# One last column unit by output halves with its column sums inside, tables, parameters and first weight unit ahead, two remainders in quarters

## The reference

```
for l in range(DEPTH):                               # DEPTH = 2
    mod = c_act @ ada_w[l] + ada_b[l]
    sh1, sc1, g1, sh2, sc2, g2 = split(mod, 6)
    h = rms_norm(x, norm1_g[l]) * (1.0 + sc1) + sh1                    # norm 1
    x = x + g1 * token_mixer(h, ..., w_in[l], ..., w_out[l])
    h = rms_norm(x, norm2_g[l]) * (1.0 + sc2) + sh2                    # norm 2
    x = x + g2 * conv_ffn(h, ffn_up[l], ..., ffn_down[l])
return rms_norm(x, final_g)
```

## Time and profile before

| what | value |
|---|---|
| median of 3 runs | 1697.12 us (1693.07 to 1697.74) |
| span of the profiled execution | 1696.2 us |
| PE busy | 1544.1 us (91%) |
| DVE busy | 718.4 us (42%) |
| ACT busy | 533.5 us (31%) |
| POOL busy | 641.6 us (38%) |
| mean granted TensorE clock | 0.946 |

### The profile page before, as it was taken

The page is one execution under the profiler, slowest core; times in us unless marked ns, Lnnn a source line. Parts: engine busy times, 40 slices in busy tenths (PEclk is TensorE's granted clock), DMA queues, the critical chain, the costliest instruction groups (busy, mean ns, idle before and its releaser), DMA issues.

```text
span 1696.2 us, 20273 instructions
## 1 busy us (share of the span) xinstructions
PE 1544.1 (91%) x7414; PEld 1222.0 (72%) x7414; DVE 718.4 (42%) x1051; ACT 533.5 (31%) x665; POOL 641.6 (38%) x283
## 2 busy tenths in 40 slices
PE   5698897899989999999968889789997999999998
PEld 5576785556868888888856778655576888888886
DVE  4879635534341122332158872654354212224211
ACT  2221332344333433321122123334442443333112
POOL 3323222211435555545513322231115455555451
PEclk7799998999979999999979989989998999999998
DMA  8575111000123333464248431100002333345431
GB/s 315 185 234 185 58 50 51 1 1 1 50 69 91 92 96 99 124 212 139 71 150 294 134 122 50 50 26 0 1 26 75 89 90 94 99 124 168 164 115 50
DMA packets 188828, 171.60 MB, mean 101 GB/s; under 512 B 15717, under 2 KB 151365, under 8 KB 188741
## 3 DMA queue, kind: packets, MB, share of 16 engines
q1 hardware_dynamic: 187572, 170.22, 31.9%
q10 hardware_dynamic: 1169, 0.25, 0.1%
HBM read 168.35 MB, written 2.10 MB: 100 GB/s over the span
## 4 chain that ended last, share of the span: by engine, by line
issue 34%; PE 25%; POOL 17%; DVE 17%; POOLq 3%; DVEq 1%; DMA 1%; ACT 1%; ACTq 0%; SPq 0%
POOL w_lo L517 13%; DVE asum L958 10%; PE psum L1361 7%; PE psum L1363 7%; PE psum L1362 7%; POOL hid_lo L584 3%; PE psum L1482 1%; PE psum L1504 1%; POOLq L569 1%; POOLq L538 1%; POOLq L570 1%; PE psum L1339 1%; POOL qm L556 1%; POOLq L533 1%; DVE asum L956 1%
## 5 line engine op out<-in xcount | busy, mean ns | idle before, releaser
L517 POOL TENSOR_TENSOR w_lo<-w_raw,w_hi 128x2048 fp32r<-128x2048 f32 x76 | 354.3, 4662 | 530.4 <-ACT w_hi L648 528.9
L648 ACT ACTIVATE w_hi<-w_raw 128x2048 fp32r<-128x2048 f32 (+2 forms) x104 | 192.9, 1855 | 652.2 <-PE psum L1363 555.9
L1361 PE MATMUL psum<-h_hi,w_hi 128*128 128x512 f32 x960 | 380.9, 397 | 5.7 <-DVE h_lo L932 4.8
L1362 PE MATMUL psum<-h_lo,w_hi 128*128 128x512 f32 x960 | 376.3, 392 | 0.0
L1363 PE MATMUL psum<-h_hi,w_lo 128*128 128x512 f32 x960 | 376.2, 392 | 0.0
L1361 PEld LDWEIGHTS psum<-h_hi,w_hi 128*128 128x128 f32 x960 | 182.1, 190 | 48.1 <-DVE h_lo L932 7.9
L1363 PEld LDWEIGHTS psum<-h_hi,w_lo 128*128 128x128 f32 x960 | 181.8, 189 | 38.8
L1362 PEld LDWEIGHTS psum<-h_lo,w_hi 128*128 128x128 f32 x960 | 182.0, 190 | 36.5
L522 POOL TENSOR_TENSOR w_lo<-w_raw,w_hi 128x1792 fp32r<-128x1792 f32 (+2 forms) x28 | 114.3, 4081 | 165.2 <-ACT w_hi L648 165.2
L1285 DVE SCALAR_TENSOR_TENSOR fy<-psum,par,fy 128x511 f32<-128x511 f32 x44 | 33.0, 750 | 325.5 <-ACT fy L840 325.5
L1363 PE MATMUL psum<-hid_hi,w_lo 128*128 128x512 f32 x352 | 140.4, 399 | 0.0
(11 more groups left out here) (234 smaller groups left out, 2139.6 us busy)
## 6 DMA issues: line engine op xcount, KB each, us to landing
w_raw<-in_ffn_up SPq DMA_DIRECT2D x88, 512.0 KB, 5.0
a_raw<-in_ada_w SPq DMA_DIRECT2D x34, 1024.0 KB, 6.6
w_raw<-in_w_in SPq DMA_DIRECT2D x48, 512.0 KB, 4.6
a_mix<-in_ada_w SPq DMA_DIRECT2D x18, 1024.0 KB, 5.3
w_raw<-in_ffn_down SPq DMA_DIRECT2D x32, 512.0 KB, 4.4
w_raw<-in_w_out SPq DMA_DIRECT2D x16, 512.0 KB, 3.9
w_raw<-in_ffn_down SPq DMA_DIRECT2D x16, 384.0 KB, 3.1
w_raw<-in_w_in SPq DMA_DIRECT2D x4, 560.0 KB, 5.2
```

The costliest lines, as they stand in the source:

```text
L517: g.tensor_tensor(w_lo[:, slot_of(u), :], w_raw[:, slot_of(u), :], w_hi[:, u % HI, :].bitcast(F32), ALU.subtract).then_inc(s_lo, 1)
L648: s.activation(w_hi[:, u % HI, 0:n], w_raw[:, r, 0:n], ACT.Copy).then_inc(s_hi, 1)
L1361: m(ps, l_hi, r_hi, start=first, stop=False)
L1362: m(ps, l_hi, r_lo, start=False, stop=False)
```

## The change

- The last unit of w_out and of ffn_down (`last_unit`) makes output half 0 for all k, signals `s_half`, and then half 1. Inside half 1 stand the column sums of the squares of chunks 0 to 5 (ahead of its last three k) and of chunk 6 (ahead of its last k). `x_update` takes chunk 6 on `s_half`.
- `sqrt_table` stands ahead of `last_squares`, no longer behind it. Unit 0 of the next layer is rounded (`high(l + 1, 0)`) and its remainder made (`low(l + 1, 0)`) ahead of the last squares.
- Units 1 and 19 are rounded inside `norm_high`, ahead of the fourth chunk (19 stood between the squares and the root, 1 behind the norm). Their remainders are made in four pieces of 512 columns with a drain between (`low_by_quarters`).
- The next layer's `parameters` are set ahead of the last update.
- In the units that follow a norm, TensorE makes the two products with `h_hi` as soon as that is there, and the third one when `h_lo` is.
- The loop over layers is written out on all engines; the inner loops stay.

```diff
+            def low_by_quarters(l, u):
+                pool.wait_ge(s_hi, l * UNITS + u + 1)
+                for i in range(4):
+                    at = slice(i * T, (i + 1) * T)
+                    last = g.tensor_tensor(w_lo[:, slot_of(u), at], w_raw[:, slot_of(u), at],
+                                           w_hi[:, u % HI, at].bitcast(F32), ALU.subtract)
+                    if i < 3:
+                        pool.drain()
+                last.then_inc(s_lo, 1)
...
-            with pool.Fori(0, L) as l:
-                low(l, 0)
+            low(0, 0)
+            for l in range(L):
                 pool.wait_ge(s_ss, 2 * l + 1)
-                low(l, 1)
+                low_by_quarters(l, 1)
...
-                low(l, 19)
+                low_by_quarters(l, 19)
...
+                if l + 1 < L:
+                    low(l + 1, 0)
...
-            def norm_high(chunks, shift):
+            def norm_high(chunks, shift, l, u):
                 for c8 in range(KD):
+                    if c8 == 3:
+                        high(l, u)
                     act.wait_ge(s_hm, chunks + c8 + 1)
...
+                sqrt_table()
                 last_squares(KD + 2 * KD * l, 2 * l + 1)
-                high(l, 19)
                 norm_root(2 * l + 1)
-                norm_high(2 * KD * l + KD, 24)
+                norm_high(2 * KD * l + KD, 24, l, 19)
...
+                if l + 1 < L:
+                    high(l + 1, 0)
+                sqrt_table()
                 last_squares(2 * KD + 2 * KD * l, 2 * l + 2, l * (AUNITS // 2) + (AUNITS + EARLY) // 2)
...
-            def x_update(l, gate, ada=None):
+            def x_update(l, gate, ada=None, ahead=None):
                 for q in range(4):
+                    if q == 3 and ahead is not None:
+                        ahead()
...
-                    unit_used(dve, l, U_OUT + q if gate == 16 else U_DOWN + 3 * q + 2)
+                    if q == 3:
+                        dve.wait_ge(s_half, 2 * l + (1 if gate == 16 else 2))
+                    else:
+                        unit_used(dve, l, U_OUT + q if gate == 16 else U_DOWN + 3 * q + 2)
                     for e in range(2):
                         c8 = 2 * q + e
+                        if c8 == KD - 1:
+                            unit_used(dve, l, U_OUT + 3 if gate == 16 else UNITS - 1)
...
-                x_update(l, 40, ada)
+                x_update(l, 40, ada, (lambda: parameters(l + 1)) if l + 1 < L else None)
...
+            def last_unit(u, banks, nk, rhs, first, n):
+                for e in range(2):
+                    for kk in range(nk):
+                        if e == 1 and kk == nk - 3:
+                            sum_squares(n, (0,))
+                        if e == 1 and kk == nk - 1:
+                            sum_squares(n, (1,))
+                        at = kk * 256 + e * P
+                        hi, lo = rhs(kk)
+                        ins = three(banks[e], w_hi[:, u % HI, at:at + P], w_lo[:, slot_of(u), at:at + P], hi, lo,
+                                    first and kk == 0, kk == nk - 1)
+                    ins.then_inc(s_used if e else s_half, 1)
+                sum_squares(n, (2,))
...
                         if f == 0:
+                            pe.wait_ge(s_hhi, l * 2 * KD + KD + kk + 1)
+                            for e in range(2):
+                                at = kk * 256 + e * P
+                                ps = pair(f % 3)[e]
+                                m(ps, w_hi[:, f % HI, at:at + P], h_hi[:, kk, :], start=kk == 0, stop=False)
+                                m(ps, w_lo[:, f % RAW, at:at + P], h_hi[:, kk, :], start=False, stop=False)
                             pe.wait_ge(s_hlo, l * 2 * KD + KD + kk + 1)
```

More of the change, by code:

```diff
@@ L268, in build @@
         s_hi, s_lo, s_used = sem("s_hi"), sem("s_lo"), sem("s_used")
+        s_half = sem("s_half")
         s_aused, s_mod = sem("s_aused"), sem("s_mod")
@@ L441, in load_up @@
                             (dst[:, :, P:2 * P], src[l, :, :, bass.ds(j * P + F, P)])])
-            with sp.Fori(0, L) as l:
-                after = sp.snap(l * -1 + (L - 1))
+            for l in range(L):
+                after = L - 1 - l
                 for u in range(RAW):
@@ L677, in _ @@
             last_squares(0, 0)
-            with act.Fori(0, L) as l:
-                high(l, 0)
+            sqrt_table()
+            high(0, 0)
+            for l in range(L):
                 norm_root(2 * l)
-                norm_high(2 * KD * l, 0)
-                high(l, 1)
+                norm_high(2 * KD * l, 0, l, 1)
                 def conv_first(c8):
@@ L978, in ada, with parameters @@
                     multiply(j, a_slot[1], asum)
[L980 to L983, removed]
-                dve.wait_ge(s_e[j], 16)
-                multiply(j, a_early[j], asum0)
-            with dve.Fori(0, L) as l:
+            def parameters(l):
                 flat = par_all[:].rearrange("p a b -> p (a b)")
@@ L999, in _ @@
                 dve.drain().then_inc(s_mod, 1)
+            dve.wait_ge(s_cact, 1)
+            for j in range(2, EARLY):
+                if j % 2 == 0 and j >= 6:
+                    dve.wait_ge(s_ag, j // 2 - 1)
+                dve.wait_ge(s_e[j], 16)
+                multiply(j, a_early[j], asum0)
+            for l in range(L):
+                if l == 0:
+                    parameters(0)
                 norm(l, 2 * l, 2 * KD * l, 0)
@@ L1391, in token_unit @@
                         b = (group * TT + t) % PB if group < 3 else t
-                        last = three(bank[b][:, 0:n], h_hi[:, k, tile], h_lo[:, k, tile],
-                                     w_hi[:, u % HI, kk * n:(kk + 1) * n], w_lo[:, slot_of(u), kk * n:(kk + 1) * n],
-                                     k == 0, k == KD - 1)
+                        ps, hi = bank[b][:, 0:n], w_hi[:, u % HI, kk * n:(kk + 1) * n]
+                        m(ps, h_hi[:, k, tile], hi, start=k == 0, stop=False)
+                        m(ps, h_hi[:, k, tile], w_lo[:, slot_of(u), kk * n:(kk + 1) * n], start=False, stop=False)
+                        if u >= 2:
+                            last = m(ps, h_lo[:, k, tile], hi, start=False, stop=k == KD - 1)
+                            if k == KD - 1 and t < TT - 1:
+                                last.then_inc(s_proj, 1)
+                    for t in range(TT if u < 2 else 0):
+                        if t == 0:
+                            pe.wait_ge(s_hlo, l * 2 * KD + k + 1)
+                        last = m(bank[t][:, 0:n], h_lo[:, k, t * P:(t + 1) * P],
+                                 w_hi[:, u % HI, kk * n:(kk + 1) * n], start=False, stop=k == KD - 1)
                         if k == KD - 1 and t < TT - 1:
@@ L1435, in _ @@
                 ada_sums(0, g, asum0)
-            with pe.Fori(0, L) as l:
+            for l in range(L):
                 spread(2 * l)
@@ L1765, in up @@
                         if f == 0:
-                            pe.wait_ge(s_hlo, l * 2 * KD + KD + kk + 1)
-                        for e in range(2):
-                            at = kk * 256 + e * P
-                            last = three(pair(f % 3)[e], w_hi[:, f % HI, at:at + P], w_lo[:, f % RAW, at:at + P],
-                                         h_hi[:, kk, :], h_lo[:, kk, :], kk == 0, kk == KD - 1)
+                            pe.wait_ge(s_hhi, l * 2 * KD + KD + kk + 1)
[4 more added lines that the diff above has]
+                                m(ps, w_lo[:, f % RAW, at:at + P], h_hi[:, kk, :], start=False, stop=False)
+                            pe.wait_ge(s_hlo, l * 2 * KD + KD + kk + 1)
+                            for e in range(2):
+                                at = kk * 256 + e * P
+                                last = m(pair(f % 3)[e], w_hi[:, f % HI, at:at + P], h_lo[:, kk, :],
+                                         start=False, stop=kk == KD - 1)
+                        else:
+                            for e in range(2):
+                                at = kk * 256 + e * P
+                                last = three(pair(f % 3)[e], w_hi[:, f % HI, at:at + P],
+                                             w_lo[:, f % RAW, at:at + P], h_hi[:, kk, :], h_lo[:, kk, :],
+                                             kk == 0, kk == KD - 1)
                     last.then_inc(s_used, 1)
```

39 lines of the change are left out of this document (25 added, 14 removed).

## The result

The changed kernel takes 1670.06 us (median of 4 runs, 1664.85 to 1682.03), the kernel before beside it on the same chip 1697.43 us (4 runs, 1693.07 to 1702.5). The ratio is 0.9836 (0.9807 to 0.9865), 27.4 us less.

The account below looks back on a forecast made before the run. TensorE loses time in gaps at the norms; behind norm 1 VectorE's modulation sums decide. Gains 7.4 + 8.6 + 1.3 - 1.1 + 1.4 = 17.6 us took the span from 1696.2 to 1678.6, median 1679.5 us; range 1672.5 to 1688.

Parts of the forecast that it names:

- Chain behind the unit: From the column unit's end to the next unit's first matmul: 2.8 + 3.64 + 1.57 us.
- The sums inside: Two groups of column sums placed inside the last column unit end it 1.9 us later, bounds 0 and 1.9.
- Norm 2, twice: Gap at norm 2 of both layers falls from 13.6 to 9.9 us: 3.7 each, 7.4 gained together.
- Norm 1 of layer 2: VectorE starts 7.3 us earlier, norm 2.9 longer, 4.17 less in the modulation sums: 8.6 us gained.
- The wait for the pieces: Inside the norm, `h_lo` beside GpSimd's quarters: 0.55 us more for about three chunks, 1.65 us.
- Norm 1 of layer 1: Start unchanged; only 4.17 - 2.9 = 1.3 us gained on VectorE.
- Final norm: No collision or waiting table to save: 8.3 against 7.3 us, a loss of 1.1 (rounded from 1.06).
- Constants in place of register arithmetic: Layer loop unrolled: 1.4 us of VectorE's 5.8 us issue gaps ahead of `asum` chains gained, nothing elsewhere.
- B: Rival: GpSimd's quarters win each time in the norm, VectorE loses 4.5 us; 7.9 gained, 1689 us, chance 0.15.
- C: Rival: clock doesn't fall in the shorter gap, or issue gaps go altogether; 1672 us, chance 0.15.
- D: Rival: slower, as the program's code doubles where the loop is unrolled; chance 0.04.
- E: Rival: no effect, sums inside the unit wait for squares, VectorE's sums take back norm 1; chance 0.04.

Follow-up runs that it names:

- a0: The changed kernel itself, timed again beside the kernel before: 1667.28 us, ratio 0.9812.
- E2: The changed kernel with all column sums behind the last unit: 1665.57 us, ratio 0.9795.
- E6: The changed kernel with all column sums behind the last unit and remainders of units 2, 3, 6, 7, 8, 9 in quarters: 1653.18 us, ratio 0.9725.
- chg: First of two traces of the changed kernel; its median was 1670.06 us in the first comparison.
- E1: The kernel before with only its layer loop written out on all five engines: 1689.7 us, ratio 0.9939.
- chg2: Second trace of the changed kernel, the slower one; the two traced executions lie 12 us apart.
- E3: The changed kernel with the remainders of units 1 and 19 as one whole GpSimd instruction each: 1681.38 us, ratio 0.9891.
- E5: The changed kernel with the remainders of units 2, 3, 6, 7, 8 and 9 in quarters too: 1663.23 us, ratio 0.9783.
- the first four experiments: The first four follow-up timings, run on one chip beside the kernel before, which took 1700.67 us there.

## Why the prediction was half right

The direction and the mechanism at the norms held, and its sum of 17.6 us was 9.8 too small against the first comparison (27.4), and 15.8 against a0 (33.4).

- **Chain behind the unit.** Forecast 8.0 us from the unit's end to the first matmul (2.8 + 3.64 + 1.57), measured 7.9 at both kinds of norm. The sums inside cost the 1.9 us put down for them: E2 and E6 show 1.7 to 2.7 a place. What I did not say is that E2 would have had the short chain without this cost.
- **Norm 2, twice.** 7.4 forecast. From `chg`, 3.4 + 1.9 and 2.7 + 2.2, less the 1.1 and 0.8 that E1 shows in the up projection: 8.3.
- **Norm 1 of layer 2.** 8.6 forecast; 7.7 and 2.1 at the spread and up to the last `asum` chains, less 0.5 that E1 has there, is 9.3. Unit 0 was ready. VectorE's norm became 13.3 us (854.26 to 867.52), 2.2 longer than 11.1 and not 2.9. This 0.7 is the gain over forecast. The wait for the pieces was sized right (1.65 forecast; 0.58 and three times 0.37 measured, 1.7); it was the late fourth chunk that cost 0.56, not 1.3.
- **Norm 1 of layer 1.** 1.3 forecast; 4.6 less E1's 2.2 is 2.4 in `chg`, and 0.2 in `chg2`.
- **Final norm.** 1.1 lost as forecast (1.3 and 0.7).
- **The step that failed: "Constants in place of register arithmetic take part of that, 0 to 5.8; I take 1.4, a quarter. Elsewhere an engine computes while it waits anyway: nothing."** E1 alone gains 11.0 us by medians (7 to 14 with its interval) and 7.7 in the stretches outside the mixers. Of this the sum held 3.0 (the turn, in norm 1 of layer 2) and 1.4. The issue gaps themselves gave back 0.9 of their 5.8; it was "elsewhere nothing" that failed. The two up projections gave 1.1 and 0.8, with TensorE's wait for `w_lo` L522 gone, and the first asum stretch and token mixer 1 are shorter as well. It is a term of the sum that was mis-sized, by 3 to 7 us.
- **What the sum left out.** One more collision, unit 9's, could go by timing alone: 4.1 us in `chg`, none in `chg2`. I had counted collisions as a fixed list read from one trace.
- **The rivals.** B, the collision moving into the norm at its full price, is refuted: `h_lo` takes 1.1 to 1.3 us beside quarters, and E3 shows the full wait (4.56 us) with whole remainders. Of C, the clock did fall (12 products at half speed instead of 8) and the gaps ahead of `asum` stayed (4.6 us in 20 places); its size, 1672, came about by other ways, and that is luck. D, the doubled code: 49 packets for 52, so no fetching was added. E: the sums inside the unit never waited.

The stretches of `chg` and `chg2` hold 27.7 and 22.9 us, and with the mixers 32.8 and 20.4. The 17.6 forecast plus 3.3 (loop), 4.3 (unit 9 and the wait behind it), 0.9 (norms 2), 0.7 (norm 1 of layer 2) and 1.1 (norm 1 of layer 1) make 27.9, against 27.7 in `chg`. This is an account of one trace: `chg2` has 2.1 us less in "asum, layer 2" and 2.2 less in "asum, layer 1". What stays open is the part of E1 between 7.7 and 11.0 us, most of which its traces have in token mixer 1, and of E3 all beyond its up projections.

## What to carry to other kernels

Where an instruction of VectorE runs beside a long one of GpSimd and both read SBUF, cut the GpSimd instruction in pieces: the wait of one instruction falls from the whole instruction's length to less than a piece's, and E6 gains 12 us over E2 with that one edit. It pays most where VectorE alternates with instructions that read PSUM (1.7 us for four pieces), and least where its instructions stand back to back (3.4 us for four pieces, 4.1 for the whole). The Trainium skill, "SBUF — State Buffer", section "Who interferes with whom", states the exclusion for a whole instruction. The rows agree (`h_lo` 4.56 us beside one of 4.58), and they add that VectorE gets in between two pieces, so that it waits for one piece only.

Work that a change moves into the busiest engine's stream costs its full time there; ask first whether it was hidden where it stood. The sums moved inside four units cost 8 to 10 us here, and with the other gains around them nobody would see it in the total. And don't price a hardware loop by its turn alone. The list of waits had one more sign of it, a short wait on an engine that should have been done, but that was 1.6 of 11 us: only the kernel with nothing but the loop written out gave the size.

## What was not expected of the hardware

- The granted clock drops in dense stretches too, for some microseconds, and not alike in each execution: 0.87, 0.91 and 1.00 from 400 to 440 us above. The kernel before went from 1692.55 us at a mean clock of 0.951 to 1709.63 at 0.942 beside the first four experiments.
- Four remainder quarters take 6.40 us beside `h_lo`, where one whole remainder takes 4.58. A piece beside VectorE's copies from PSUM takes 1.27 us in E5 with 0.14 between two, so about half of the 1.8 is the cutting and half the waiting for VectorE. In the changed kernel it was hidden; in E5 TensorE waits 7.0 us in four places for such remainders, where the changed kernel waits 3.0 in two.
- An event of 4 us on VectorE can hang on a microsecond: unit 9's remainder fell beside the last chain of layer 2 in one trace of the changed kernel, and of E1, and into it in the other. With unit 9 in quarters the median stayed where it was.
